# Two-layer diffusion trunk on one core: shared experts' stage and projection pieces in another order

## What is computed

```python
for l in range(DEPTH):
    mod = silu(c) @ w_mod[l] + b_mod[l]            # 6 rows of 1024; another set for the context
    h = modulate(rms_norm(x, norm_mix[l]), sh1, sc1)
    u = split_cols(h @ w_in[l])
    # a: grouped-query, b: neighbourhood, c: differential, d: latent attention; 4 heads each
    x = x + g1 * (concatenate([a_lat, b_lat, c_lat, d_lat]) @ w_out[l])
    h2 = modulate(rms_norm(x, norm_ffn[l]), sh2, sc2)
    x = x + g2 * moe_ffn(h2, ...)
...
def moe_ffn(h, ...):
    scores = sigmoid(xs @ router_w)      # best group of 4, in it the best 2 of its experts
    out = swiglu(xs, ws_gate, ws_up, ws_down)                        # the shared expert
    for e in range(16):
        out = out + gates[:, e:e+1] * swiglu(xs, w_gate[e], w_up[e], w_down[e])
    return out
```

## Time and profile before

| | |
|---|---|
| median of three runs | 1700.93 us (1700.41 to 1703.8) |
| the profiled execution's own time | 1706.32 us |
| its span, first to last instruction | 1704.1 us |
| mean granted clock of TensorE | 0.975 of full speed |
| PE busy | 1557.8 us, 91% |
| DVE busy | 844.0 us, 50% |
| ACT busy | 429.2 us, 25% |
| POOL busy | 197.5 us, 12% |

### The profile page before, as it was taken

How to read it: one execution, slowest core, us unless ns; L and a number is a source line. 1 busy time by engine, 2 the same in 40 slices (tenths; PEclk the granted TensorE clock), 3 DMA queues, 4 the chain that set the end, 5 groups by cost and what they waited for, 6 DMA issues and landing times.

```text
span 1704.1 us, 24238 instructions
## 1 busy us (share of the span) xinstructions
PE 1557.8 (91%) x8946; PEld 1017.6 (60%) x8946; DVE 844.0 (50%) x1797; ACT 429.2 (25%) x922; POOL 197.5 (12%) x350
## 2 busy tenths in 40 slices
PE   4999999899999999899999599999899999899992
PEld 3655445666665476677776355555565666677771
DVE  1222534566766566455555521434667655544444
ACT  1312113455544310000000222113455541000001
POOL 0110102000000000112121210202000000112112
PEclk8999999999999999999999799999999999999996
DMA  9574230501001486388887673442301034478874
GB/s 336 195 265 149 100 49 1 186 1 38 13 26 50 140 331 236 130 325 323 310 317 277 228 255 132 138 72 52 140 1 38 13 108 166 185 292 301 317 287 159
DMA packets 107613, 284.76 MB, mean 167 GB/s; under 512 B 32256, under 2 KB 41918, under 8 KB 93118
## 3 DMA queue, kind: packets, MB, share of 16 engines
q1 hardware_dynamic: 97150, 262.48, 43.8%
q0 software_dynamic: 10368, 20.99, 3.3%
HBM read 265.47 MB, written 38.80 MB: 179 GB/s over the span
## 4 chain that ended last, share of the span: by engine, by line
PE 82%; DMA 6%; DVE 3%; issue 3%; SPq 3%; ACT 1%; POOL 0%; DVEq 0%; POOLq 0%; ACTq 0%
PE S L1173 16%; PE S L1490 12%; PE B L1306 9%; PE S L1241 9%; PE S L1500 6%; PE PT L1258 5%; PE B L1289 5%; DMA arena<-in_moe_w_up 5%; PE B L1192 3%; PE B L1086 2%; PE PT L1395 2%; PE S L1192 2%; PE PT L1484 1%; PE S L1371 1%; PE S L1378 1%
## 5 line engine op out<-in xcount | busy, mean ns | idle before, releaser
L1173 PE MATMUL S<-arena 128*128 128x512 f32 (+3 forms) x768 | 299.4, 540 | 3.9 <-ACT arena L852 3.9
L1490 PE MATMUL S<-arena 128*128 128x256 f32 x1152 | 260.0, 382 | 11.7 <-DMA arena<-in_moe_w_up 8.3
L1490 PEld LDWEIGHTS S<-arena 128*128 128x128 f32 x1152 | 218.6, 191 | 60.4 <-issue 32.8
L1173 PEld LDWEIGHTS S<-arena 128*128 128x128 f32 x768 | 141.5, 192 | 125.5 <-issue 104.9
L956 ACT ACTIVATE arena<-S,nmax 128x768 f32<-128x768 f32 (+1 forms) x200 | 162.0, 813 | 160.3 <-DVE nmax L1926 119.7
L1926 DVE TENSOR_REDUCE nmax<-S 128x1 f32<-128x768 f32 (+1 forms) x168 | 133.2, 826 | 83.8 <-PE S L1241 83.6
L1241 PE MATMUL S<-arena 64*128 64x256 f32 (+5 forms) x720 | 162.1, 500 | 10.4 <-ACT arena L956 8.6
L1306 PE MATMUL B<-arena 128*128 128x512 f32 x320 | 156.4, 618 | 2.5 <-DVE arena L1980 1.8
L1258 PEld LDWEIGHTS PT<-cst,arena 128*128 128x128 f32 x832 | 93.9, 141 | 83.9 <-issue 65.1
L1258 PE MATMUL PT<-cst,arena 128*128 128x128 f32 x832 | 121.0, 277 | 24.0 <-ACT arena L956 11.7
L1500 PE MATMUL S<-arena 128*128 128x512 f32 x288 | 129.9, 594 | 2.4 <-DVE arena L2064 2.4
(11 more groups left out here) (283 smaller groups left out, 1747.7 us busy)
## 6 DMA issues: line engine op xcount, KB each, us to landing
arena<-in_w_mod SPq DMA_DIRECT2D x24, 2048.0 KB, 9.6
arena<-in_moe_w_gate SPq DMA_DIRECT2D x36, 1024.0 KB, 6.7
arena<-in_moe_w_up SPq DMA_DIRECT2D x36, 1024.0 KB, 9.6
arena<-in_moe_w_down SPq DMA_DIRECT2D x36, 1024.0 KB, 6.8
arena<-in_w_in SPq DMA_DIRECT2D x6, 2048.0 KB, 10.9
arena<-y SPq DMA_DIRECT2D x20, 512.0 KB, 8.2
arena<-mod SPq DMA_DIRECT2D x16, 512.0 KB, 16.4
arena<-in_tokens SPq DMA_DIRECT2D x12, 512.0 KB, 9.4
```

What stands on the lines that cost most here:

```text
L1173: mm = pe.matmul(ubank[u % 4][:, c0:PANEL_W[p]], hT[:, k, t * P:(t + 1) * P], panel[p][:, k, c0:], start=k == 0, stop=k == KT - 1)
L1490: mm = pe.matmul((S0, S1)[b][:, 512 * w:512 * w + DE], XT[b][:, k, :], wgu[b][:, w, k * DE:(k + 1) * DE], start=k == 0, stop=k == KT - 1)
```

## The change

It has three groups of edits.

1. Attention: pieces start at step 0 and not at step 2; the order of the chunks and the waits of a piece follow, each on its own chunk. The last tile's first five pieces go into the two steps behind its last score (`LAST_PIECES`).
2. Shared experts' stage, layer 0: the two scalings write to two tiles, `swd_g2[0]` and the down weights themselves, and move up into DVE's loop over tiles, with DVE's wait for weights and gate rows ahead of that loop. The product of tile 4 has bank S0. The first expert's transposes stand ahead of tile 5's product, and DVE's copy of them ahead of the last output sum. `route_weights` moves back by one tile.
3. Counts are read earlier on every engine; on GpSimd ahead of the wait for the table. On SP the input panel of the next layer (layer 0) and the expert down weights (layer 1) wait for the indices of the first two gathers.

```diff
-PIECES = {2: (0, 3), 3: (3, 6), 4: (6, 7), 5: (7, 8), 6: (8, 11), 7: (11, 14), 8: (14, 15), 9: (15, 16)}
+PIECES = {0: (0, 1), 1: (1, 2), 2: (2, 4), 3: (4, 6), 4: (6, 7), 5: (7, 8), 6: (8, 11), 7: (11, 14), 9: (14, 16)}
+LAST_PIECES = {0: (0, 4), 1: (4, 5)}
-CHUNK_ORDER = [0, 1, 4, 6, 7, 2, 3, 5]
+CHUNK_ORDER = [0, 2, 6, 3, 4, 1, 7, 5]
...
-        swd_g2 = [a.rearrange("p (a b) -> p a b", a=2) for a in (hT2_all, hT2_more[:, 2 * D:4 * D])]
+        swd_g2 = [arena[:, take.at[0]:take.at[0] + 2 * D].rearrange("p (a b) -> p a b", a=2), swd]
...
-            return (S1 if t == T - 1 else PT) if l == 0 else (PT, S1)[t % 2]
+            return {4: S0, 5: S1}.get(t, PT) if l == 0 else (PT, S1)[t % 2]
...  SP
                     sp.wait_ge(s["mod_mm"], NMCH + 4)
+                    sp.wait_ge(s["e_idx"], 2)
                     win_load(1, 0)
...
-                    for b in range(2):
-                        w_load(b, b)
+                    e0, e1 = expert_of(0), expert_of(1)
+                    in_load(0, 0, e0)
+                    in_load(1, 1, e1)
+                    sp.wait_ge(s["e_idx"], ge(0) + 2)
+                    down_load(0, e0)
+                    down_load(1, e1)
...  PE, out_piece
-                        if c == 0:
-                            pe.wait_ge(s["o_v"], V_JOBS * g(t) + V_JOBS)
                         pe.wait_ge(s["res_mul"], 2 * g(t) + c)
-                    if at_ == 2:
-                        pe.wait_ge(s["d_fin"], FINALS * g(t) + 1)
-                    if at_ == KT - 1:
-                        pe.wait_ge(s["d_fin"], FINALS * g(t) + 2)
+                    if c == 0:
+                        kind, i = [job for job in CHUNK if CHUNK[job] == j][0]
+                        if kind == "c":
+                            pe.wait_ge(s["d_fin"], FINALS * g(t) + i + 1)
+                        else:
+                            pe.wait_ge(s["o_v"], V_JOBS * g(t) + V_JOB_NO[kind, i] + 1)
...  PE, the steps
-                    pieces = range(*PIECES[k]) if t and t < nt and k in PIECES else []
-                    if n == NS + 2:
+                    in_step = PIECES if t < nt else LAST_PIECES
+                    pieces = range(*in_step[k]) if t and k in in_step else []
+                    if n == NS:
...
-                for piece in range(2 * KT):
+                for piece in range(LAST_PIECES[1][1], 2 * KT):
                     out_piece(nt - 1, piece)
...  PE, shared stage
-                    if l == 0 and 1 <= t < nt - 1:
+                    if l == 0 and 1 <= t < 4:
                         pe.wait_ge(s["s_ob"], g(t))
...
+                        if t == nt - 1:
+                            pe.wait_ge(s["s_ob"], gend - 2)
+                            e_turn(0, 0, 0, True)
                         s_down(t)
...
-                pe.wait_ge(s["s_ob"], gend - 1)
-                e_turn(0, 0, 0, l == 0)
+                if l:
+                    pe.wait_ge(s["s_ob"], gend - 1)
+                    e_turn(0, 0, 0, False)
...  GpSimd
+                pairs, _, pairs_2 = pair_counts(pool, l)
                 pool.wait_ge(s["h2_stored"], 16 * gend)
                 pool.wait_ge(s["r_slots"], l + 1)
-                pairs, _, pairs_2 = pair_counts(pool, l)
...  DVE
+                dve.wait_ge(s["s_w_in"], 16 * 4 * (l + 1))
+                dve.wait_ge(s["s_g2_in"], 16 * 3 * (l + 1))
                 if l:
-                    dve.wait_ge(s["s_w_in"], 16 * 4 * 2)
-                    dve.wait_ge(s["s_g2_in"], 16 * 3 * 2)
-                    dve.wait_ge(s["h2_ready"], gend)
                     s_scale_down(0)
                 for t in range(2, nt):
                     s_half(t)
                     s_gate_mul(t - 2)
+                    if l == 0 and t >= 4:
+                        s_scale_down(t - 4)
...
                     s_up_mul(1)
-                    s_scale_down(0)
                     route_experts()
...
                         if t == 3:
                             modcol_of(1, B6)
-                            route_weights()
+                            pairs, pairs_1, pairs_2 = pair_counts(dve, l)
+                        if t == nt - 1:
+                            x_half(0, 0)
                         s_out(t)
...
                         if t == 3:
-                            s_scale_down(1)
+                            route_weights()
```

51 lines of the change are left out of this document (28 added, 23 removed).

## The result

The change makes the kernel faster. In the first measurement the median of four runs is 1686.26 us (1684.61 to 1687.66) against 1701.26 us for the kernel before (1700.41 to 1703.8). The ratio is 0.9909, with a 95% interval from 0.9892 to 0.9926. In a second measurement (`change_again`) the ratio was 0.9865 (0.9839 to 0.9892), with medians of 1683.13 and 1705.01 us. The two intervals just meet, so the gain is best given as 12.6 to 27 us, with 15 in the first and 22 in the second medians. The forecast was 1683.4 us.

The account below looks back on a forecast made before the run. The prediction took TensorE (PE), 82% of the span, as the bound and its idle time as the question; -5.5 - 3.4 + 0.1 - 5.5 - 1.8 - 1.4 = -17.5 us from 1700.9 gave 1683.4 us, range 1679 to 1687 (52 in 100).

Parts of the forecast that it names:

- Shared stage, layer 0: PE's waits of 3.38 us before tile 4's product and 2.10 us before the first expert's gate product go: -5.5 us.
- The +0.1 for a late `s_up_mul(1)`: Layer 0's shared stage: this multiply runs about 1 us late and PE's modulation product waits for it, +0.1 us.
- the forecast 4: Layer 0's first gather: in SBUF at 681.2, PE asks at about 685.5, which leaves 4 us.
- The clock of the first gate product: First expert in layer 0: with the clock staying at 2.4 GHz the gate product takes 3.62 us, -1.8 us.
- Shared stage, layer 1: The gather is issued 1.9 us sooner, so PE's wait of 1.41 us for it goes: -1.4 us.
- Steps of the tiles: Attention tiles: moving projection pieces between steps gives -0.6 us a tile, -3.0 in layer 0 and -1.8 in layer 1.
- The rival that the tiles give nothing: Attention tiles: idle time at the boundaries may be chain, so they gain nothing; 1688.2 us, 15 in 100.
- The end of layer 0's attention: Last tile's early pieces cover waits, -1.4 us, or -2.6 with clock recovery; tiles and end together taken as -5.5.
- The 2.57 us of clock: Layer 0's last output projection: first half 9.70 us against 7.13 for the second, the difference put down to the clock.
- the cap that I had named: End of layer 0's attention: h2 loads limit PE's gain to at most 2.0 + 3.4 = 5.4 us.
- in 12 and not 16 instructions: Sign of being right: the last tile's pieces run in 12 instructions, not 16, at a clock of 1.00.
- The end of layer 1's attention: Five early pieces of the last tile cover PE's waits of 1.18 and 0.38 us: -1.6 us.

Follow-up runs that it names:

- change_again: The changed kernel once more, unchanged, measured against the kernel before: ratio 0.9865, median 1683.13 us.
- transposes_behind: The changed kernel with the first expert's transposes in layer 0 behind the last down product again: ratio 0.9905 to the kernel before.
- attention_only: The kernel before with the attention edits alone: ratio 0.9959 to the kernel before.
- no_waits_on_sp: The changed kernel without SP's two waits for the gathers' indices, so input panel and expert down weights go ahead of the gathers: ratio 0.9909 to before.
- before_again: The kernel before, unchanged, run once more for a second profile: 1701.86 us.
- no_tail: The changed kernel with the last tile's sixteen pieces in one row again, none early: ratio 0.9895 to the kernel before.
- tail_split: The changed kernel with the last tile's first four pieces split, two ahead of the last transposes and two behind them: ratio 0.9857 to the kernel before.

## Why the prediction was right

The forecast of 1683.4 us stood 2.9 us from the first median. The sign held, and so did most places and mechanisms: PE's idle times went where the trace had shown them. Three sizes did not hold. Part of the closeness is luck: the end of layer 0's attention gave 2.5 us less than its term, layer 1's shared stage 2 to 3.5 us more.

- *Shared stage, layer 0* (-5.5): S0 is 5.9 us shorter than in the profiled execution that I read, 7.4 to 7.6 shorter than in the two others without these edits. The difference is the clock behind the 3.38 us: the product of tile 4 took 3.67 us in that one execution and 5.24 and 5.37 in the others. `transposes_behind` shows that 1.9 us of it come from the order of the transposes alone. The +0.1 for a late `s_up_mul(1)` did not show: PE's wait there is 1.30 us before and after. The first gather was issued 1.9 us sooner against the table product, as forecast, and landed 5.8 us before PE asked for it, for the forecast 4.
- *The clock of the first gate product* (-1.8): 6.1 to 4.33 us, -1.8. It was not certain before either (4.42 for G0 in one execution of three), but in eleven profiles with the shared edits the stretches S0 and G0 hold no slow product, and in all three without them one or two. The Trainium skill, TensorE: Matmul & The Clock Gate, section What's actually happening, says that the number of slow matmuls at the start of one kernel varies from run to run; the two executions of the kernel before show the like in its middle, with 3.0 us between them in E0.
- *Shared stage, layer 1* (-1.4): -3.3 on the executions with a slow down product (29.4 and 29.5 to 26.1), -4.9 where the clock stayed up (30.16 to 25.22). **The term was mis-sized.** I took the 1.41 us of the earlier trace rows for the gather's price; it was what a slow down product had left of it. The gather itself set 13.6 us from the table product on. That distance fell in two steps: the early counts brought it to 12.5 us (`attention_only` against `no_waits_on_sp`, -1.1), the down weights moved behind the gather to 9.5 (-2.95). I had costed the second at nothing. At full clock there was no more to gain from the first gather: the second landed just as PE asked for it.
- *Steps of the tiles* (-0.6 each, -4.8 together): T0 -3.2, T1 -2.3, together -5.5 for the forecast -4.8. Tile by tile in layer 0 it is 1.4, 0.45, 0.46, 0.15 and 0.8 us. For tiles 2 and 3 my count from the rows was -0.4, and step by step it fits: step 1 +0.15 (for +0.2), steps 2 and 3 together -0.95 (for -0.8), step 8 -0.19 (for -0.34), step 9 +0.55 (as forecast). Of the 5.5, 0.86 in each layer come back in E0 and E1 with the last tile's step 9, so by the prediction's own count of whole tiles the steps give about 3.8. The rival that the tiles give nothing is refuted.
- *The end of layer 0's attention* (what was left of -5.5, 2.5 us): E0 26.19 to 29.07 with the pieces, 26.20 and 26.59 at full clock without: nothing. **This step failed, in three terms.** The 2.57 us of clock were chance; `before_again` had the full clock without any change. The waits that the early pieces were to cover were put at 1.4 us; between the second executions of both kernels only waits of 0.64 and 0.38 us went, one of 0.88 grew by 0.17, and the 0.86 us of the moved piece take up the rest, so that the last piece ends 23.2 us behind the last score, for 23.3 before. And the cap that I had named was lower than I set it: the store of h2 did not stay where it was but came later against the last score by as much as the pieces stand ahead of ACT's copy, so the loads were issued 1.4 us sooner on the clock, not 2, and PE could begin 7.3 us behind the first issue in the profiled execution and 6.0 in the second. `no_tail` and `tail_split` show that the wait comes from these pieces: without them, or with two of them moved, PE waits for no load. At full clock it cost little, since PE's old wait of 1.12 us ahead of the gate product went as the 1.11 us for the loads came; behind the 2.39 us the clock fell too. Of the signs, the last tile's pieces "in 12 and not 16 instructions" was miscounted: the first half's are 8 in a row.
- *The end of layer 1's attention* (-1.6): -0.8 to -1.1, with the 0.86 us of the moved piece in it.

With the stretches of the profiled pair the sum is -3.2 - 0.2 - 5.9 - 1.8 - 2.3 - 0.8 - 4.2 = -18.4 us against the -17.5 forecast; with the second pair, whose E0 and S1 fell differently, -3.2 + 0.3 - 7.4 - 1.8 - 2.2 - 1.1 - 3.4 = -18.8. Both lie between the two measurements. The spans of the profiled pair differ by 20.7 us; another 2.6 of them lie in X, for which the sum has no term. Those of the second pair differ by 18.4, with X the same.

## What to carry to other kernels

An idle time ahead of a transfer's consumer is not the transfer's price: count from the event that allows the transfer to its consumer, in two executions, before saying what an earlier issue is worth. Work that fills an idle time also delays everything behind it on its engine, so put it behind what feeds a store, as the split of the last pieces did. And where several transfers share the engines, the order of issue is part of the critical path even across queues: 1 MB moved ahead of a store cost 5 us here with the clock behind it, and two loads moved behind a gather gave 3.

## What the runs showed of the hardware

In fourteen executions the granted clock of TensorE fell near the same kinds of places, behind waits of 0.4 to 4.7 us, but not in each of them: the product behind layer 0's wait of 3.38 us took 3.67, 5.24 and 5.37 us in three executions of the same order, and the down product of layer 1, behind two waits of 0.7 us, 3.68 us in four executions and 5.38 to 6.54 in ten. A window on one of them, the second execution of the kernel before (start and end, length, busy time of PE, PEld, DVE, ACT, POOL, granted clock, DMA share, GB/s):

```profile
1464.70:1470.70 6.00, 6.00 (x9) 2.55 (x10) 3.43 (x12) 0.00 (x0) 1.72 (x3) 0.58 1.02 427
```

PE has no idle time in it, and the clock is 0.58 of full: mostly 1.2 GHz, the lower of the two levels. Two executions of one kernel thus differ by 3 us in one stretch of 26, more than most single terms of this change. The tiles' steps, T0 and T1, repeat to 0.05 us, though PE waits up to 1.18 us in them. To judge a term of 1 us, one execution of each kernel is enough only in stretches that have been seen to repeat.
